# Weight slots moved 128 bytes, so that TensorE's two operands lie 64 instead of 192 bytes apart modulo 256, and the recurrence's last low part computed directly behind its gate

## The chip, the cores and the metric

The kernel runs on one core of a Trainium2 chip. The metric is the device time of one execution in microseconds (us). Before the change it is 815.14 us, the median of three runs (814.79 to 816.20 us).

## What is computed

One transformer-like block of 272 tokens (16 meta tokens and 256 others) with a model width of 1024, followed by two further layers on the 256 tokens, all in float32:

```
first_block:  a = rms_norm(h);  columns = split(a @ w_in)            # 1024 x 7680
              y_na = neighbourhood_attention(q, k, v) @ w_na_out
              y_hg = hgrn2_branch(q, z_fwd, z_bwd, i, g) @ w_hg_out  # the recurrence, both directions
              h = h + (sigmoid(gate_na)*y_na + sigmoid(gate_hg)*y_hg) @ w_o
              h = h + square(relu(rms_norm(h) @ w_up)) @ w_down
even_layer:   a, u, v, gate = split(ada(h) @ even_in);  pool mixer, spatial gating;  h += gate_res * (y @ even_out)
odd_layer:    ... = split(ada(h) @ odd_in);  gated linear attention, stick-breaking attention;  h += gate_res * (y @ odd_out)
out = rmsnorm(h)
```

The end of the recurrence branch is `o = o * rsqrt(mean(o*o)) * gain * silu(g)` per head, four heads of 128 rows. It is called the gate below. Its result is the input of `@ w_hg_out`.

## The kernel before

**Weights.** All weight matrices are cut into 259 units of 128 x 1024 numbers. SyncE's queue fetches a unit from HBM into one of six `raw` buffers. ScalarE (ACT) rounds it to TensorE's fp32r format (`wh`, the high part, line 205 of the profile, the helper `copy`), and VectorE (DVE) subtracts that from the original (`wl`, the low part, line 235, the helper `tensor_tensor`). Each activation that is multiplied is split in the same way into a high and a low part (XAh and XAl, B0h and B0l, B1h and B1l, XUh and XUl). A product is then three matmuls, Xh by wl, Xh by wh and Xl by wh, each with 128 x 128 stationary numbers and 256 moving ones per row (272 in the first stages, 258 in the stages "a" and "qk"). A full unit is 24 matmuls.

**Slots.** `wh` and `wl` have five slots (NSPLIT) of 1056 numbers, of which a unit takes 1024: it starts at the slot's number 0 or at its number 32, which is 128 bytes further. `half(j)` chooses. Unit j lies in slot j mod 5. A slot is 4224 bytes long, which is 16 times 256 and 128 more, so that neighbouring slots start 128 bytes apart modulo 256, and the choice evens that out.

**Roles.** In most stages the weights are the stationary operand and the activations move. In the stages that `streams(j)` names (the value rows v, i, vn, gv and sv) it is the other way round.

**Addresses.** From the order and the sizes of the buffers, the start addresses modulo 256 within a partition are: wh and wl 128, XAh and XAl 0, XUh, XUl, B0h, B0l, B1h and B1l 64. Most stages read XA from its number 16 on, which is at 64. So before the change a stationary weight is at 128 and the moving activation at 64: the moving operand lies 192 bytes past the stationary one modulo 256. In the `streams` stages the weights move and are at 0, the activation is stationary at 64, and the distance is again 192. Three places differ. The stage zf reads XA from its number 0 (distance 128). In the rows v the second slice of tokens starts at number 144 of XUh, which is at 128 (distance 0 - 128, or 128). In "a" and "qk" a row block of B1 or B0 is 264 numbers, 1056 bytes, long, so that the distance grows by 32 bytes with each of the eight blocks and takes all of 192, 224, 0, 32, 64, 96, 128 and 160.

**Order.** Every engine runs the same walk over the units. After each unit it takes one or two steps of a side program (attention, recurrence and others) by `next()` on a Python generator: what stands between two `yield`s is issued in one step. VectorE and ScalarE prepare the weights of a unit three and four units ahead (AHEAD, LEAD), between the steps. The order on an engine is thus fixed by the place of the `yield`s. The side program `recurrence` ends on VectorE with a loop over the four heads: the gate of head hh (`ro_gated`, line 223), the low part of the head before (`hg_low(hh - 1)`, line 235) and a `yield`; `hg_low(3)` comes behind the loop. `hg_low(hh)` waits for ScalarE's high part B0h of the same head. TensorE's stage "hg" multiplies by w_hg_out, and each of its row blocks waits for the high and the low part of one head.

Of the kernel before, what the change touches and what calls it, by code (L numbers as in the profile page):

```python
# [108 lines left out]
def bc(ap, dims):  # L109

    return bass.AP(ap.tensor, ap.offset, [list(ap.ap[0])] + [list(d) for d in dims])
# [21 lines left out]
class Counts:  # L133
# [17 lines left out]
    def up(self, name, *events):  # L151
        key = SHARE.get(name, name)
        assert self.by.setdefault(key, self.owner) == self.owner, name
        self.n[key] = self.last[name] = self.n.get(key, 0) + 1
        for ev in events:
            assert not self.known or self.value[name, ev] == self.n[key], (name, ev)
            self.value[name, ev] = self.n[key]
        return self.of(name), 1

    def at(self, name, event):  # L160
        return self.of(name), self.value[name, event] if self.known else self.value.get((name, event), 1)

    def now(self, name):
        return self.of(name), self.last[name]
# [150 lines left out]
def in_turn(*runs):  # L315

    runs = list(runs)
    while runs:
        for r in list(runs):
            try:  # L320
                next(r)
            except StopIteration:
                runs.remove(r)
                continue
            yield
# [6 lines left out]
def build(nc, ws, par, cst, msk, xt, xk, biasd, negwd, late, bsd, wtd, crd, out):  # L332
# [4 lines left out]
    with ExitStack() as ctx:  # L337
# [186 lines left out]
        def bk(*key):  # L524
            return banks[bank_of[key]] if c.known or key in bank_of else banks[0]
# [27 lines left out]
        def wide(x, g):  # L553
            return x[:, 2 * g:2 * g + 2, :]
# [16 lines left out]
        def streams(j):  # L571

            _, name, _, _, col, _ = items[mats[j]]
            return any(name == n and c0 <= col < c1 for n, c0, c1 in (
                ("w_in", 1024, 1536), ("w_in", 3072, 3584), ("even_in", 2048, 3072), ("odd_in", 1024, 2048),
                ("odd_in", 4112, 5136)))

        def half(j):
            n = j % NSPLIT
            o = 32 if n % 2 != streams(j) else 0  # L580
            return wh[:, n, o:o + 1024], wl[:, n, o:o + 1024]

        def last_unit(name, k0, c):
# [8 lines left out]
        def last_of(v, b, i):  # L592
            x = v[:, :, i:i + 1]
            return bass.AP(x.tensor, x.offset, [list(x.ap[0]), list(x.ap[1]), [0, b]])

        def halves(a, b):
            v = a.rearrange("p h (g two b) -> p (h g) two b", two=2, b=b)
            return v[:, :, 0, :], v[:, :, 1, :]
# [4 lines left out]
        def scores(b, hh):  # L603

            v = AT[:, 2 * hh:2 * hh + 2, :].rearrange("p h (a c) -> p h a c", c=128)
            return v[:, :, 1:3, :] if b == 128 else v[:, :, 0::3, :]
# [1343 lines left out]
        def vector_program(e):  # L1950
# [286 lines left out]
            def recurrence():  # L2237
                yield

                def levels(g):  # L2240
                    TF, TB = SF[g], EP[g]
                    F_, B_, KF, KB = (wide(z, g) for z in (ff, fb, kf, kb))
                    lev = -1
                    for b in LEVELS:
                        if b == 0:
                            e.tensor_tensor(Xl[g][:, :, :], KF, KB, ALU.add).then_inc(*up("xl", g))
                        elif b < 256:
                            fh, bh, tf, tb = (halves(z, b) for z in (F_, B_, TF[:, :, :], TB[:, :, :]))
                            if b == 1:
                                e.wait_ge(*at("factors", g))  # L2250
                            e.wait_ge(*at("xy", (g, b, 0)))
                            x = e.tensor_tensor(fh[1], fh[1], last_of(tf[0], b, 0), ALU.mult)
                            if b < 128:
                                x.then_inc(*up("f_new", (g, b, 0)))
                                e.wait_ge(*at("xy", (g, b, 1)))
                                e.tensor_tensor(bh[0], bh[0], last_of(tb[1], b, 0), ALU.mult).then_inc(
                                    *up("f_new", (g, b, 1)))
                                e.wait_ge(*at("k_up", (g, b)))
                                e.wait_ge(*now("f_new"))
                                for z in (tf, tb):  # L2260
                                    x = e.tensor_tensor(z[0][:, :, 0:1], z[0][:, :, 0:1], z[1][:, :, 0:1], ALU.mult)
                            x.then_inc(*up("f_up", (g, b)))
                        yield
                        if b > 64:
                            continue
                        src = bk("level", g, b)[:, :].rearrange("p (h t c) -> p h t c", h=2, t=2)
                        e.wait_ge(*at("level", (g, b)))
                        if b == 0:
                            e.wait_ge(*at("masks", 0))
                            x = e.tensor_copy(scores(b, g), src)  # L2270
                        else:
                            e.wait_ge(*now(f"at_diag"))
                            x = e.copy_predicated(scores(b, g), bc(K8[:, lev, :], [[0, 2], [0, 2], [1, 128]]), src)
                        x.then_inc(*up("at_diag", (g, b)))
                        lev += 1

                yield from in_turn(levels(0), levels(1))
                for hh in range(4):
                    e.wait_ge(*at("ro", hh))
                    e.tensor_copy(oS[hh], bk("ro", hh)[:, 0:256]).then_inc(*up("ro_copy", hh))  # L2280
                    yield
                    yield
                yield
                for hh in range(4):
                    e.wait_ge(*at("ro_normed", hh))
                    e.wait_ge(*at("silu", ("g", hh)))
                    e.scalar_tensor_tensor(oS[hh], oS[hh], hp[:, hh:hh + 1], sg[:, hh, :], ALU.mult,
                                           ALU.mult).then_inc(*up("ro_gated", hh))
                    if hh:
                        hg_low(hh - 1)  # L2290
                    yield
                hg_low(3)

            def hg_low(hh):
                low((B0h[:, 4 + hh, 0:256], B0l[:, 4 + hh, 0:256]), oS[hh], ("hg_high", hh), "hg_low", hh)

            w.side.append(recurrence())
            w.steps = 1
            rows("i", "w_in", 3072, 3584)
# [423 lines left out]
            for g in range(4):  # L2723
                b, k = g // 2, 4 * (g % 2)
                n = slice(128 * b, 128 * b + 128)
# [362 lines left out]
```

## Time and profile before

| | before |
|---|---|
| median of three runs | 815.14 us |
| the profiled execution, its own time | 816.26 us |
| its span in the profile | 814.3 us |
| TensorE busy (PE) | 800.0 us, 98% of the span |
| VectorE busy | 641.3 us, 79% |
| ScalarE busy | 501.2 us, 62% |
| GpSimd busy | 110.2 us, 14% |
| matmuls | 6996 |
| share of PE in the chain that ended last | 96% |
| granted TensorE clock, mean | 0.999 |

PE is busy in nearly every slice of the span. Since matmuls are pipelined, one lasts about 278 ns from its start to its modelled end while the next starts far earlier. The busy time therefore does not show how fast TensorE works. The distance from one start to the next does: it can be read in the timeline, or from the number of matmuls in a window.

### The profile page before, as it was taken

What the parts mean: (1) busy time and instruction counts of PE and PEld (TensorE: products, weight loads), DVE (VectorE), ACT (ScalarE), POOL (GpSimd) and SP (SyncE); (2) the same over time, 40 slices, a digit from 0 to 9 for tenths busy, and PEclk for the clock granted to TensorE, in tenths of its full rate; (3) what the DMA queues carried; (4) which work ended last, traced back from release to release, by engine and by line L of the source; (5) the groups of instructions that cost most, each with busy time, mean ns of one, the idle gap of its engine ahead of it and who ended that gap; (6) DMA issues with size and microseconds to landing.
All of it is one profiled execution on the core that took longest, in us unless ns stands there. A gap on an engine that the chain in (4) does not pass through costs nothing.

```text
span 814.3 us, 17246 instructions
## 1 busy us (share of the span) xinstructions
PE 800.0 (98%) x6996; PEld 789.3 (97%) x6996; DVE 641.3 (79%) x1032; ACT 501.2 (62%) x899; POOL 110.2 (14%) x133
## 2 busy tenths in 40 slices
PE   6999999999999999999999999999999999999996
PEld 6999999999999999999999999999999999999996
DVE  7788599977977878787998898887997568566673
ACT  6576667756567464656676844555686467566652
POOL 0022265401030000000230300001203130000001
PEclk9999999999999999999999999999999999999999
DMA  9934543566666989888777666675665446455441
GB/s 338 386 97 138 178 131 131 156 202 212 201 185 226 360 305 334 310 316 328 259 256 228 210 189 217 216 257 188 207 182 156 133 129 193 176 155 155 150 129 52
DMA packets 47021, 170.41 MB, mean 209 GB/s; under 512 B 5216, under 2 KB 5472, under 8 KB 46688
## 3 DMA queue, kind: packets, MB, share of 16 engines
q1 hardware_dynamic: 46224, 165.31, 61.5%
q10 hardware_dynamic: 720, 4.01, 1.2%
q8 instruction: 56, 0.92, 0.5%
q14 instruction: 21, 0.17, 0.1%
HBM read 168.26 MB, written 1.05 MB: 208 GB/s over the span
## 4 chain that ended last, share of the span: by engine, by line
PE 96%; DVE 1%; ACT 1%; DMA 1%; POOL 1%; issue 0%; SPq 0%; POOLq 0%; DVEq 0%; ACTq 0%
PE bank L196 95%; DMA raw<-in_ws 1%; POOL sq L235 1%; PE bank L199 0%; DVE wl L235 0%; SPq L193 0%; ACT wh L205 0%; ACT sq L202 0%; ACT B1h L202 0%; DVE gd L235 0%; DVE h L223 0%; DVE h L235 0%; POOLq L337 0%; DVEq L337 0%; DVE vt L235 0%
## 5 line engine op out<-in xcount | busy, mean ns | idle before, releaser
L235 DVE TENSOR_TENSOR wl<-raw,wh 128x1024 fp32r<-128x1024 f32 (+1 forms) x260 | 326.6, 1268 | 20.9 <-ACT wh L205 19.8
L205 ACT CAST wh<-raw 128x1024 fp32r<-128x1024 f32 (+1 forms) x260 | 269.7, 1047 | 101.4 <-PE bank L196 50.6
L196 PE MATMUL bank<-XAh,wl 128*128 128x256 f32 (+1 forms) x896 | 254.7, 284 | 0.0
L196 PE MATMUL bank<-XAl,wh 128*128 128x256 f32 (+1 forms) x896 | 249.3, 278 | 0.0
L196 PE MATMUL bank<-XAh,wh 128*128 128x256 f32 (+1 forms) x896 | 249.2, 278 | 0.0
L196 PEld LDWEIGHTS bank<-XAh,wl 128*128 128x128 f32 x896 | 168.3, 188 | 2.1 <-issue 0.7
L196 PEld LDWEIGHTS bank<-XAl,wh 128*128 128x128 f32 x896 | 168.9, 189 | 0.0
L196 PEld LDWEIGHTS bank<-XAh,wh 128*128 128x128 f32 x896 | 168.8, 188 | 0.1
L196 PE MATMUL bank<-B1h,wl 128*128 128x256 f32 (+1 forms) x464 | 129.4, 279 | 0.0
L196 PE MATMUL bank<-B1l,wh 128*128 128x256 f32 (+1 forms) x464 | 128.8, 278 | 0.0
L196 PE MATMUL bank<-B1h,wh 128*128 128x256 f32 (+1 forms) x464 | 128.8, 278 | 0.0
L235 POOL TENSOR_TENSOR sq<-sq 128x256 f32<-128x256 f32 x37 | 42.4, 1146 | 505.6 <-ACT sq L202 503.3
L196 PE MATMUL bank<-B0l,wh 128*128 128x256 f32 (+1 forms) x392 | 108.8, 278 | 0.0
L196 PE MATMUL bank<-B0h,wh 128*128 128x256 f32 (+1 forms) x392 | 108.7, 278 | 0.0
L196 PE MATMUL bank<-B0h,wl 128*128 128x256 f32 (+1 forms) x384 | 108.1, 282 | 0.0
L196 PEld LDWEIGHTS bank<-B1l,wh 128*128 128x128 f32 x464 | 87.5, 188 | 0.0
L196 PEld LDWEIGHTS bank<-B1h,wl 128*128 128x128 f32 x464 | 87.3, 188 | 0.1
L196 PEld LDWEIGHTS bank<-B1h,wh 128*128 128x128 f32 x464 | 87.3, 188 | 0.1
L196 PEld LDWEIGHTS bank<-B0h,wh 128*128 128x128 f32 x392 | 73.8, 188 | 0.1
L196 PEld LDWEIGHTS bank<-B0l,wh 128*128 128x128 f32 x392 | 73.8, 188 | 0.0
L196 PEld LDWEIGHTS bank<-B0h,wl 128*128 128x128 f32 x384 | 72.3, 188 | 0.5 <-issue 0.3
L223 DVE SCALAR_TENSOR_TENSOR raw<-raw,crow 128x1024 f32<-128x1024 f32 x48 | 58.5, 1219 | 0.0
(280 smaller groups left out, 1209.5 us busy)
## 6 DMA issues: line engine op xcount, KB each, us to landing
raw<-in_ws SPq DMA_DIRECT2D x306, 512.0 KB, 4.5
bias<-in_bias ACTq DMA_DIRECT2D x1, 1664.0 KB, 12.2
hK<-in_xk SPq DMA_DIRECT2D x4, 272.0 KB, 5.1
h<-in_xt ACTq DMA_DIRECT2D x1, 1088.0 KB, 7.4
out<-gd SPq DMA_DIRECT2D x4, 256.0 KB, 2.6
raw<-in_ws SPq DMA_DIRECT2D x2, 256.0 KB, 3.9
C<-in_cst SPq DMA_DIRECT2D x1, 512.0 KB, 8.3
crow<-in_crow ACTq DMA_DIRECT2D x1, 512.0 KB, 5.8
```

The lines of the kernel that those rows point to most:

```text
L196: return self.real.matmul(*a, **k)
L205: return self.real.copy(*a, **k)
L223: return self.real.scalar_tensor_tensor(*a, **k)
L235: return self.real.tensor_tensor(*a, **k)
```

## The change

```
 def half(j):
     n = j % NSPLIT
-    o = 32 if n % 2 != streams(j) else 0
+    o = 32 if n % 2 == streams(j) else 0
     return wh[:, n, o:o + 1024], wl[:, n, o:o + 1024]
```

Every unit now lies in the other half-place of its slot. Stationary weights are at 0 modulo 256 instead of 128, moving weights at 128 instead of 0. The distance from the stationary to the moving operand is 64 instead of 192 in both roles. In zf it becomes 0, in the second slice of the rows v also 0, and in "a" and "qk" the same eight distances come in a rotated order. No instruction is added, removed or moved by this.

```
                     if hh:
                         hg_low(hh - 1)
-                    yield
+                    if hh < 3:
+                        yield
                 hg_low(3)
```

The last `yield` of the gate's loop is gone, so `hg_low(3)` is issued in the same step as the gate of head 3 and `hg_low(2)`. On VectorE, at the end of the stage "na" and "g20", just ahead of "hg", the order of before (-) and after (+) is as follows. Xl<-Xl,hp,sg is a gate, B0l<-Xl,B0h a low part of a head, wl<-raw,wh the low part of a unit of weights, ghg<-ghg,bank the first work on a product of w_hg_out.

```order
 L235 TENSOR_TENSOR B0l<-Xl,B0h 128x256
 L223 SCALAR_TENSOR_TENSOR Xl<-Xl,hp,sg 128x256
-L235 TENSOR_TENSOR B0l<-Xl,B0h 128x256
-L235 TENSOR_TENSOR wl<-raw,wh 128x1024
-L235 TENSOR_TENSOR B0l<-Xl,B0h 128x256
-L235 TENSOR_TENSOR wl<-raw,wh 128x1024
+L235 TENSOR_TENSOR B0l<-Xl,B0h 128x256 x2
+L235 TENSOR_TENSOR wl<-raw,wh 128x1024 x2
 L223 SCALAR_TENSOR_TENSOR ghg<-ghg,bank 128x256 x2
```

The low part of head 3 has moved ahead of one low part of weights. Nothing else changes its place on any engine.

## Rows read from the trace of the kernel before

**Rows 1.** Page, parts 1 and 4: busy us; chain by engine.
```profile
PE 800.0 (98%) x6996; PEld 789.3 (97%) x6996; DVE 641.3 (79%) x1032; ACT 501.2 (62%) x899; POOL 110.2 (14%) x133
PE 96%; DVE 1%; ACT 1%; DMA 1%; POOL 1%; issue 0%; SPq 0%; POOLq 0%; DVEq 0%; ACTq 0%
```

**Rows 2.** Windows: us, busy time and (x matmuls in flight) of each engine, clock, DMA.
```profile
205.00:249.00 44.00, 44.00 (x376) 44.00 (x375) 35.58 (x58) 28.88 (x52) 8.46 (x7) 1.00 0.61 188
255.00:405.00 150.00, 150.00 (x1326) 150.00 (x1325) 122.19 (x172) 88.75 (x147) 4.02 (x3) 1.00 0.87 314
423.00:434.00 11.00, 11.00 (x94) 11.00 (x93) 10.83 (x24) 8.59 (x15) 0.00 (x0) 1.00 0.62 187
457.00:481.00 24.00, 24.00 (x206) 24.00 (x206) 23.66 (x38) 16.39 (x31) 1.80 (x2) 1.00 0.70 230
520.00:576.00 56.00, 56.00 (x497) 56.00 (x496) 46.20 (x73) 32.12 (x51) 6.12 (x5) 1.00 0.65 214
606.00:624.00 18.00, 18.00 (x161) 18.00 (x161) 16.30 (x22) 13.03 (x20) 4.93 (x5) 1.00 0.54 171
662.00:690.00 28.00, 28.00 (x249) 28.00 (x248) 22.20 (x34) 19.56 (x34) 7.15 (x8) 1.00 0.53 162
691.00:778.00 87.00, 87.00 (x720) 86.18 (x719) 55.13 (x84) 57.23 (x103) 0.00 (x0) 1.00 0.52 163
780.00:800.00 20.00, 20.00 (x179) 20.00 (x178) 11.65 (x16) 9.07 (x14) 3.21 (x3) 1.00 0.19 60
```

**Rows 3.** Timeline of PE, stage "hg" (start us, us, engine line op out<-in).
```profile
202.71 0.28 PE L196 MATMUL bank<-B0h,wl 128*128 128x256 f32 x1
...
203.27 0.28 PE L196 MATMUL bank<-B0l,wh 128*128 128x256 f32 x1
203.43 0.36 PE L196 MATMUL bank<-B0h,wl 128*128 128x256 f32 x1
203.62 0.28 PE L196 MATMUL bank<-B0h,wh 128*128 128x256 f32 x1
203.74 0.28 PE L196 MATMUL bank<-B0l,wh 128*128 128x256 f32 x1
203.86 0.28 PE L196 MATMUL bank<-B0h,wl 128*128 128x256 f32 x1
```

**Rows 4.** Timeline of DVE, the same place.
```profile
201.00 0.47 DVE L223 SCALAR_TENSOR_TENSOR Xl<-Xl,hp,sg 128x256 f32<-128x256 f32 x1
201.40 0.41 DVE L235 TENSOR_TENSOR B0l<-Xl,B0h 128x256 fp32r<-128x256 f32 x1
201.73 1.21 DVE L235 TENSOR_TENSOR wl<-raw,wh 128x1024 fp32r<-128x1024 f32 x1
202.87 0.41 DVE L235 TENSOR_TENSOR B0l<-Xl,B0h 128x256 fp32r<-128x256 f32 x1
203.20 1.21 DVE L235 TENSOR_TENSOR wl<-raw,wh 128x1024 fp32r<-128x1024 f32 x1
204.41 0.42 DVE L223 SCALAR_TENSOR_TENSOR ghg<-ghg,bank 128x256 f32<-128x256 f32 x1
```

**Rows 5.** Timeline of ACT: the high part of head 3.
```profile
201.51 0.41 ACT L205 CAST B0h<-Xl 128x256 fp32r<-128x256 f32 x1 [0.32 <-DVE Xl L223]
```

**Rows 6.** Timeline of PE, rows v: pairs of matmuls, distance 192, then 128.
```profile
34.13 0.39 PE L196 MATMUL bank<-wh,XUl 128*128 128x256 f32 x2
...
34.81 0.39 PE L196 MATMUL bank<-wh,XUl 128*128 128x256 f32 x2
35.04 0.39 PE L196 MATMUL bank<-wl,XUh 128*128 128x256 f32 x2
...
36.22 0.41 PE L196 MATMUL bank<-wh,XUl 128*128 128x256 f32 x2
```

**Rows 7.** Timeline of PE: 272 columns, distance 192 (XU), then 128 (XA in zf).
```profile
15.08 0.29 PE L196 MATMUL bank<-XUh,wh 128*128 128x272 f32 x1
...
16.56 0.29 PE L196 MATMUL bank<-XUh,wh 128*128 128x272 f32 x1
...
54.17 0.28 PE L196 MATMUL bank<-XAh,wh 128*128 128x272 f32 x1
...
55.69 0.29 PE L196 MATMUL bank<-XAh,wh 128*128 128x272 f32 x1
```

**Rows 8.** Timeline of PE where the rows vn end and the stage "ga" begins.
```profile
456.12 0.39 PE L196 MATMUL bank<-wh,XAl 128*128 128x256 f32 x2
456.35 0.28 PE L196 MATMUL bank<-XAh,wl 128*128 128x256 f32 x1
456.46 0.28 PE L196 MATMUL bank<-XAh,wh 128*128 128x256 f32 x1
456.58 0.28 PE L196 MATMUL bank<-XAl,wh 128*128 128x256 f32 x1
456.70 0.28 PE L196 MATMUL bank<-XAh,wl 128*128 128x256 f32 x1
456.82 0.28 PE L196 MATMUL bank<-XAh,wh 128*128 128x256 f32 x1
```

**Rows 9.** Page, part 5: how long the weights' preparation takes on DVE and ACT.
```profile
L235 DVE TENSOR_TENSOR wl<-raw,wh 128x1024 fp32r<-128x1024 f32 (+1 forms) x260 | 326.6, 1268 | 20.9 <-ACT wh L205 19.8
L205 ACT CAST wh<-raw 128x1024 fp32r<-128x1024 f32 (+1 forms) x260 | 269.7, 1047 | 101.4 <-PE bank L196 50.6
```

More of the change, by code:

```diff
@@ L579, in half @@
             n = j % NSPLIT
-            o = 32 if n % 2 != streams(j) else 0
+            o = 32 if n % 2 == streams(j) else 0
             return wh[:, n, o:o + 1024], wl[:, n, o:o + 1024]
```

## The prediction

> **What bounds the kernel now.** I read the page first. PE is busy for 98% of the span, and the chain that ended last is 96% PE [rows 1]. No transfer and no other engine is long on that chain, so only what changes the pace of TensorE, or makes it wait, can move the time. Busy time says nothing of the pace, so next come windows in stages with one kind of matmul. A window counts a matmul that is in flight at its edge, and one lasts 278 ns, so I take 2.4 off each count. From 255 to 405 us that leaves 1323.6 in 150 us, or 113.3 ns from start to start. The windows 520:576, 606:624, 662:690 and 780:800 give 113.2 to 113.5 [rows 2]. From 205 to 249 us it is 44 us by 373.6, or 117.8 ns, and 457:481 gives 24 by 203.6, or 117.9 [rows 2]. I call these the fast and the slow pace. The two differ by 4.5 ns, or 4%, with the same 256 columns, the same buffers, the same distance of 192 and a granted clock of 1.00 in both. The 258-column window gives 11 by 91.6, or 120.1 ns [rows 2].
>
> The timeline shows how the pace changes. In "hg" it is fast until 203.27. The next matmul starts at 203.43 and the one after it at 203.62. From there the starts are 0.12 apart [rows 3], and the window from 205 on is slow to its end. After 255 us it is fast for 150 us without a break. So a pace, once taken, is kept for long, and an interruption can change it. That is not all: at 456.46 it turns slow at the border of two stages, where no gap stands [rows 8]. The operands' addresses alone do not set it, since both paces occur at one distance.
>
> **Part one, the last low part.** Why does PE stop at 203.3? It starts the row block of head 3 there, which needs B0l of that head. VectorE ends this low part at 202.87 + 0.41 = 203.28, since 1.21 us of weights stand ahead of it (201.73) [rows 4]. The two starts from 203.27 to 203.62 take 0.35 us where two at the fast pace take 0.227, so the stop costs 0.12 us [rows 3]. In the changed order the low part comes behind the one of head 2, which ends at 201.81 [rows 4]. It waits for ScalarE's high part, which ends at 201.51 + 0.41 = 201.92 [rows 5]. It then ends near 202.4, and PE wants it at 203.3: 0.9 us to spare. The stop is gone, -0.12 us.
>
> What is queued behind the moved instruction pays. The low part of weights that began at 201.73 begins near 202.4, 0.6 us later. It is prepared three units ahead, and a unit of 24 matmuls lasts 2.7 to 2.8 us, so it has over 5 us to spare. The raw buffer that it frees is refilled 0.6 us later, with six buffers in turn. The next low part of weights (203.20) and the first ghg (204.41) come at most 0.4 us later [rows 4], since VectorE does the same work in total. The products of "hg" fill four banks and none is wanted back before "o" starts, so I cost this at nothing. Were a delay to reach PE, it would be below 0.6 us.
>
> The larger term hangs on the pace. If PE is not stopped, it should carry the fast pace through "hg", "o" and "up0", until the sum of squares at 249.3 interrupts it. From 203.6 to 249.2 are 45.6 us at 117.8 ns, or 387 matmuls. At 113.3 ns they save 387 * 4.5 ns = 1.74 us. The bounds of this term are 0 (it turns slow anyhow, as in rows 8) and -1.8.
>
> **Part two, the distance of 64.** No instruction is added. ScalarE writes and VectorE reads and writes a place 128 bytes off, for 1047 and 1268 ns a unit [rows 9]. Against a unit on PE of 2.7 us this is covered, and nothing in the trace ties those times to an address. What may change is the pace of PE. No stage runs at 64 for long, so I bound it by the nearest rows.
>
> On the side of a loss: in the rows v, matmuls at distance 192 go from 34.13 to 34.81 in 0.68 us for 6, or 113.3 ns. The next slice of tokens, at distance 128, takes from 35.04 to 36.22 for 10, or 118 ns [rows 6]. With 272 columns the distance 192 gives 1.48 / 12 = 123.3 ns and 128 gives 1.52 / 12 = 126.7 [rows 7]. So a distance can cost 3 to 5 ns. The stages "a" and "qk" go through all eight distances, 64 among them, and never reach the 114 ns that two more columns than 256 would ask for: 120.1 [rows 2]. A fast pace at full length is seen at 192 alone. If 64 never lets the fast pace come, the price is 4.5 to 6.8 ns a matmul. The fast windows of rows 2 add up to 272 us. I estimate 130 us more in stretches shared with the recurrence and both attentions, together some 3,500 matmuls: +16 to +24 us.
>
> On the side of a gain: if 64 never lets the slow pace come, the slow stretches 203.6 to 249.2 and 456.3 to 516, and an estimated half of 691:778 (720 matmuls in flight, mixed) [rows 2], are about 149 us, of which 3.8% are 5.7 us. The 1.7 us of part one are in that. The stages now at 120 ns could give up to 3 us more. So this side ends near -9 us.
>
> Between +24 and -9 I take zero, since the rows give no sign for 64. The range of whole-length windows at 192 already holds both paces, so the distance is at most one cause among several, and 64 is 192 read backwards (the stationary operand 192 past the moving one). The interruptions would then deal the paces anew, each by luck. One slow stretch of the size seen (387 matmuls, or some 500 from 456 to 516) is 1.7 to 2.3 us, so this case spreads by about 2.5 us both ways.
>
> The page "SBUF — State Buffer" of the Trainium skill says, in "Who interferes with whom", that TensorE has two independent SBUF read ports, one for the moving operand and one for the weight load. By that rule no distance could matter and only part one would be left. The step from 113.3 to 118 ns in rows 6, with nothing changed but the slice of tokens, speaks against it, though an interruption would do the same. In "TensorE: Matmul & The Clock Gate", under "Wait — 56ns, not 53.3ns?", the skill gives 2.5 ns beyond columns / 2.4 GHz, an estimate of 109.2 ns for 256 columns. The trace does not agree: 113.3 at best. By the page even the fast pace holds 4 ns of something else.
>
> **The sum.** The profiled execution took 816.26 us (span 814.3 and 2 us around it), 1.1 above the median of the runs. -0.12 for the stop, -1.74 for the pace behind it and 0 for the distance make -1.9 us: 814.4 for that execution and **813.2** against the median of 815.14.
>
> **The rivals.**
> - *64 is a bad distance.* Two reads then meet in most matmuls, and slow becomes the rule. Half of the 3,500 fast matmuls turned slow give +7.9 - 0.1 = 823 us, all of them 831, and at the pace of 120.1 it is 839. For it speak rows 6 and 7, and that 192 alone shows fast. Against it, rows 6 are one place behind an interruption. It is slower than before as soon as some 450 fast matmuls more are slow than the 387 that part one frees: one long stage.
> - *64 is a good distance.* The slow pace goes, -5.7 - 0.1 = 809.3 us, down to 806 if the stages at 120 ns gain too. For it speaks that 192 is evidently not free of the slow pace; against it, no row.
> - *Only the stop goes.* The pace turns slow at "hg" or "o" anyhow, as it does at 456.46 without a gap [rows 8], and the distance does nothing: -0.12, or 815.0 us. This is also what is left if the offset does not do what it says because the period is 128 and not 256 bytes.
>
> **How the numbers follow.** My forecast (paces dealt anew, "hg" to "up0" fast) gets 0.44, with a range of its own of 810.5 to 816. The bad distance gets 0.28, the good one 0.18, only the stop 0.10. A measurement of this kernel can tell about 0.2%, or 1.6 us, from no change, so faster means below 813.5. The forecast lies just beyond that and gives 0.28 to faster, 0.11 to the same and 0.05 to slower. With the good distance faster is 0.46. With only the stop the same is 0.21. With the bad distance slower is 0.33. The range is 806.5 to 831. It leaves out the half of the bad case at which the pace falls below 117.8 (about 0.1) and little at the lower end.
>
> **What would show it.** Step one is right if the DVE timeline shows B0l of head 3 ending near 202.4 and PE has no gap at 203.3. Step two is right if a window from 205 to 249 us holds about 390 matmuls instead of 376. The distance is neutral if the window of 150 us in "up" and "down" still holds about 1326, and the slow stretches elsewhere are as long as before, though in other places. It is a bad distance if that window falls to 1275 (slow) or 1250 (120 ns), and a good one if 457:481 rises from 206 to 214. The prediction is wrong if the stretch between 250 and 400 us changes its pace, since then the distance and not the interruptions decides.

## The result, and the profile after

The changed kernel takes 830.89 us, the median of four runs (830.67 to 831.31), against 815.11 us for the kernel before on the same chip. The ratio on record is 1.0176, with a 95% interval from 1.0135 to 1.0217 (the two medians by themselves give 1.0194). The forecast of 813.2 us was wrong. What came is the rival "64 is a bad distance" at the price it had with all fast matmuls turned slow, 831 us, which was the upper end of the range.

The profiled execution took 831.03 us with a span of 829.0 us, 14.7 us more than the span before. Of the page, first the busy times of part 1, then the chain of part 4, then the two lines on the weights' preparation:

```profile
PE 815.2 (98%) x6996; PEld 804.6 (97%) x6996; DVE 641.9 (77%) x1032; ACT 499.3 (60%) x899; POOL 110.3 (13%) x133
PE 98%; DMA 0%; POOL 0%; DVE 0%; ACT 0%; issue 0%; SPq 0%; DVEq 0%; ACTq 0%; POOLq 0%
L235 DVE TENSOR_TENSOR wl<-raw,wh 128x1024 fp32r<-128x1024 f32 (+1 forms) x260 | 326.7, 1268 | 22.8 <-ACT wh L205 21.7
L205 ACT CAST wh<-raw 128x1024 fp32r<-128x1024 f32 (+1 forms) x260 | 268.4, 1042 | 106.4 <-PE bank L196 58.7
```

Against [rows 1] PE has the same 6996 matmuls and is busy for 15.2 us longer. The other engines do the same work in the same time. The preparation of the weights takes 1268 and 1042 ns a unit, as in [rows 9]. So no longer wait shows there, and TensorE itself is slower. The windows, with the columns of [rows 2], say where:

```profile
205.00:249.00 44.00, 44.00 (x376) 44.00 (x375) 36.35 (x60) 27.98 (x48) 8.49 (x7) 1.00 0.62 193
255.00:405.00 150.00, 150.00 (x1276) 150.00 (x1275) 115.63 (x165) 84.98 (x146) 0.17 (x1) 1.00 0.86 310
457.00:481.00 24.00, 24.00 (x209) 24.00 (x208) 21.18 (x33) 18.50 (x34) 5.80 (x7) 1.00 0.66 210
520.00:576.00 56.00, 56.00 (x476) 55.95 (x476) 44.77 (x76) 29.53 (x46) 1.57 (x1) 1.00 0.64 212
662.00:690.00 28.00, 28.00 (x233) 27.79 (x233) 18.93 (x28) 17.63 (x29) 7.97 (x9) 1.00 0.50 146
780.00:800.00 20.00, 20.00 (x168) 19.89 (x167) 16.50 (x28) 11.02 (x16) 0.00 (x0) 1.00 0.52 158
```

The 150 us of "up" and "down" hold 1276 matmuls where [rows 2] have 1326. With 2.4 taken off, that is 150 / 1273.6 = 117.8 ns from start to start, the slow pace, at a granted clock of 1.00 as before. The windows 520:576, 662:690 and 780:800 fall from 497, 249 and 179 to 476, 233 and 168. That is more than the pace alone, since each stage now begins 8 to 14 us later and part of such a window lies in the stage ahead of it. By the start stamps the stages themselves run at 117.8 ns, without a break from 525 to 587 and from 792 to 817 us. Those that were slow before stay as they were: 205:249 holds 376 again, and 457:481 goes from 206 to 209, since it is fast up to 464.4 us.

From the start stamps of the whole trace, by the mean of three neighbours: of some 5,600 matmuls by weights with 256 columns, about 4,000 ran at 113 to 115 ns before and 1,300 at 117 to 119. After the change it is about 620 and 4,700. The mean of the 5,500 steps that hold no stop (below 150 ns) goes from 114.59 to 117.29 ns, and 2.70 ns * 5,500 = 14.9 us, which is the whole difference of the spans. Matmuls with 258 columns (120.3 and 120.2 ns) and with 272 (125.7 and 126.0) have no part in it.

The end of the recurrence on DVE and the high part on ACT, with the columns of [rows 4] and [rows 5], then PE at the same place:

```profile
202.79 0.47 DVE L223 SCALAR_TENSOR_TENSOR Xl<-Xl,hp,sg 128x256 f32<-128x256 f32 x1
203.19 0.97 DVE L235 TENSOR_TENSOR B0l<-Xl,B0h 128x256 fp32r<-128x256 f32 x2
204.07 1.22 DVE L235 TENSOR_TENSOR wl<-raw,wh 128x1024 fp32r<-128x1024 f32 x1
```

```profile
203.29 0.41 ACT L205 CAST B0h<-Xl 128x256 fp32r<-128x256 f32 x1 [0.33 <-DVE Xl L223]
```

```profile
203.55 0.28 PE L196 MATMUL bank<-B0h,wh 128*128 128x256 f32 x1
203.66 0.28 PE L196 MATMUL bank<-B0l,wh 128*128 128x256 f32 x1
203.78 0.28 PE L196 MATMUL bank<-B0h,wl 128*128 128x256 f32 x1
...
204.49 0.28 PE L196 MATMUL bank<-B0h,wl 128*128 128x256 f32 x1
```

The last two low parts now stand in one row of DVE, x2, and end at 204.16, 0.46 us behind the high part. PE goes on in steps of 0.12 us with no stop like the one in [rows 3]. It has nothing to lose there, since it was slow already.

### The profile page after: what moved, and what is told of

Its sections match the earlier page's. It is cut to its first block, busy times and chain, and to the rows that moved or that the text cites. A ratio compares the mean times of both kernels' runs of the same rounds, so it can differ in the third digit from the quotient of the medians.

```text
span 829.0 us, 17246 instructions
## 1 busy us (share of the span) xinstructions
PE 815.2 (98%) x6996; PEld 804.6 (97%) x6996; DVE 641.9 (77%) x1032; ACT 499.3 (60%) x899; POOL 110.3 (13%) x133
## 4 chain that ended last, share of the span: by engine, by line
PE 98%; DMA 0%; POOL 0%; DVE 0%; ACT 0%; issue 0%; SPq 0%; DVEq 0%; ACTq 0%; POOLq 0%
PE bank L196 97%; DMA raw<-in_ws 0%; PE bank L199 0%; POOL sq L235 0%; DVE gd L235 0%; ACT B1h L202 0%; SPq L193 0%; DVEq L337 0%; ACT sq L202 0%; DVE wl L235 0%; ACT wh L205 0%; DVE h L235 0%; DVE h L223 0%; ACT rsB L202 0%; ACT lnb L202 0%
## 5 line engine op out<-in xcount | busy, mean ns | idle before, releaser
L235 DVE TENSOR_TENSOR wl<-raw,wh 128x1024 fp32r<-128x1024 f32 (+1 forms) x260 | 326.7, 1268 | 22.8 <-ACT wh L205 21.7
L205 ACT CAST wh<-raw 128x1024 fp32r<-128x1024 f32 (+1 forms) x260 | 268.4, 1042 | 106.4 <-PE bank L196 58.7
```

The costliest lines, as they stand in the source:

```text
L205: return self.real.copy(*a, **k)
L235: return self.real.tensor_tensor(*a, **k)
```

## The experiments

Ratios are those on record, against runs of the kernel before on the same chip. They are not the quotients of the two medians, and differ from them by up to 0.4%. A pace is the mean time from one matmul's start to the next.

**The two parts apart.** *low_only* undoes the flip of the slots and keeps the low part behind its gate:

```
-            o = 32 if n % 2 == streams(j) else 0
+            o = 32 if n % 2 != streams(j) else 0
```

> Only the last low part of the recurrence is moved behind its gate; the distance stays at 192. Theory A (the distance of 64 makes the slow pace of 117.8 ns the rule, the low part only removes a stop): the stop of 0.12 us at 203.3 goes, and the fast pace of 113.3 ns is carried on to 249 us, 813.2 us, about 1.9 below before; a window from 205 to 249 us holds about 390 matmuls. Rival B (the pace turns slow at this place anyhow): about 815.0 us, 376 matmuls. Rival C (the changed order of VectorE is what made the changed kernel slower): 825 us or more.

It took 814.62 us (814.28 to 815.31, 11 runs) against 814.87, ratio 0.999 (0.9972 to 1.0008). Its DVE, its PE and two windows:

```profile
201.33 0.47 DVE L223 SCALAR_TENSOR_TENSOR Xl<-Xl,hp,sg 128x256 f32<-128x256 f32 x1
201.72 0.98 DVE L235 TENSOR_TENSOR B0l<-Xl,B0h 128x256 fp32r<-128x256 f32 x2
202.62 2.35 DVE L235 TENSOR_TENSOR wl<-raw,wh 128x1024 fp32r<-128x1024 f32 x2
```

```profile
203.28 0.28 PE L196 MATMUL bank<-B0l,wh 128*128 128x256 f32 x1
203.39 0.28 PE L196 MATMUL bank<-B0h,wl 128*128 128x256 f32 x1
203.50 0.28 PE L196 MATMUL bank<-B0h,wh 128*128 128x256 f32 x1
```

```profile
205.00:249.00 44.00, 44.00 (x389) 43.95 (x388) 37.06 (x61) 29.99 (x54) 8.48 (x7) 1.00 0.60 199
255.00:405.00 150.00, 150.00 (x1326) 150.00 (x1325) 122.01 (x175) 87.11 (x144) 4.68 (x3) 1.00 0.87 314
```

In the trace this is the first part as predicted: the low part is done by 202.7, the stop is gone and the fast pace goes on through "hg", 389 matmuls where 376 were. The profiled span is 812.8 against 814.3 us, -1.5 us. The time is not as predicted. The medians differ by 0.25 us, within their interval, where 1.9 us were expected. The next pair of kernels shows why.

*dist64_only* is the complement. It keeps the flip and puts the last `yield` back.

> Only the slots are moved, so that the distance is 64; the low part stays in its old place. Theory A (the distance makes the loss): 830 to 832 us, window 255 to 405 us with about 1276 matmuls. Rival C (the loss needs the moved low part): about 815 us.

It took 830.95 us (ratio 1.0197, 1.0181 to 1.0212), with 1276 matmuls from 255 to 405 us, as expected. The flip alone does all the damage.

**Place or distance.** The flip also moves the weights. *acts_moved_64* leaves them at 128 and moves the activations by 128 bytes, which gives a distance of 64. *both_moved_192* has both the flip and the shift, and so a distance of 192 with the weights at 0. Both kernels keep the last `yield` where it was before the change. The shift:

```
         wl = sbt(ctx, "wl", [128, NSPLIT, 1056], F32R)
+        sbt(ctx, "shift", [128, 32])
         XAh = sbt(ctx, "XAh", [128, 8, 320], F32R)
```

> The weights stay where they are before the change (stationary at 128 modulo 256), but all buffers behind them, the activations among them, lie 128 bytes further, so that the distance from the stationary to the moving operand is 64. Theory A (the distance counts): as slow as the changed kernel, 829 to 833 us. Rival D (the absolute place of the weights at 0 instead of 128 counts, for instance for the engines that write them): 815 us.

> Weights at their new place (stationary at 0 modulo 256) and all buffers behind them 128 bytes further too, so that the distance is again 192. Theory A (the distance counts): 812 to 818 us, with the fast pace of 113.3 ns in most of the window 255 to 405 us. Rival D (the absolute place counts): 829 to 833 us.

They took 830.84 us (1.0194, 1.018 to 1.0208) and 814.83 us (1.0001, 0.9975 to 1.0027), with 1276 and 1326 matmuls in the long window. Between these four pairs of places, 128 bytes apart, the distance decides and the place does not.

*both_moved_192* also answers the question that *low_only* left. It has the old order on DVE, and so the stop of PE at head 3, here at 203.94 us. Yet the stretch behind the stop is fast:

```profile
203.81 0.28 PE L196 MATMUL bank<-B0l,wh 128*128 128x256 f32 x1
203.94 0.36 PE L196 MATMUL bank<-B0h,wl 128*128 128x256 f32 x1
204.13 0.28 PE L196 MATMUL bank<-B0h,wh 128*128 128x256 f32 x1
205.00:249.00 44.00, 44.00 (x388) 43.95 (x388) 36.78 (x61) 29.64 (x53) 8.47 (x7) 1.00 0.63 196
```

The last line is the window with the columns of [rows 2]: 388 matmuls, as many as *low_only* has without the stop. So the stop does not by itself make this stretch slow. The profiled execution of the kernel before, 816.26 us, was slow there. *both_moved_192* was fast there at 815.12, and most executions of the kernel before lie near 814.9. That they were fast in this stretch too is inferred, since none of them was profiled. It would explain why taking the stop away leaves the median as it is.

**Which stages.** *stationary_64* has `o = 32 if n % 2 == 0 else 0`, which gives 64 to the stages with stationary weights alone. *moving_64* has `n % 2 == 1`, which gives it to the rows alone.

> Only the stages in which the weights are stationary get the distance 64 (the slots start at their number 32 in slots 0, 2 and 4 for every unit); the rows stages keep 192. Theory A1 (the loss is all in the stages with stationary weights, since the rows vn and gv ran at 113.3 ns at 64 in the changed kernel's trace): 830 to 832 us. Rival (each stage loses by its share of the matmuls, the rows stages hold about an eighth): 828 to 829 us.

> Only the rows stages, in which the weights move, get the distance 64; all others keep 192. Theory A1: 814 to 816 us, no change. Rival (share of the matmuls): about 817 us.

*stationary_64* took 831.64 us (1.02, 1.0183 to 1.0217), so the stages with stationary weights hold the loss. *moving_64* took 814.68 us (0.9998, 0.9964 to 1.0033). Its profiled execution took 821.86 us, and shows something else:

```profile
255.00:405.00 150.00, 150.00 (x1276) 150.00 (x1275) 117.25 (x164) 84.49 (x141) 1.37 (x1) 1.00 0.85 307
```

"up" and "down" lie at 192 in this kernel, and here they ran at 117.8 ns from 249.7 to 416.3 us, 1,414 matmuls with 256 columns, behind the sum of squares at 249.2. 1,414 * 4.5 ns = 6.4 us, most of the 7.2 us to its median. So 192 does not secure the fast pace. The kernel before has such executions too. Its runs lie at some 814 to 817 or at 822 to 824, and in one set of runs 13 of 22 were in the upper group. No execution of it in the upper group was profiled, so that its cause is the same is inferred from *moving_64*.

Other slow stretches do not change from kernel to kernel. By the stamps the 214 matmuls from about 456 to 481 us are slow in the kernel before, *low_only*, *both_moved_192* and *place32_192* alike, and so are 44 matmuls near 492 and 68 near 508. In *moving_64* the rows "vn" ahead of the first of them lie at 64, and there it is fast (463 to 487 us). That is one execution, and it suggests that what stood before has a part in the choice.

**Other distances in the kernel.** *dist0*, *dist128* and *dist32* use the shift with 16, 16 (with the flip) and 24 numbers.

> The slots as before, and all buffers behind the weights 64 bytes further, so that both operands start at the same place modulo 256 (distance 0). Theory A (a place of its own for each distance; 192 is the good one): between 819 and 840 us, since the second slice of the rows v and zf ran at 118 and 126.7 ns at 128. Rival E (only odd and even multiples of 64 differ, or the period is 128): 0 behaves as 128 does, and 64 as 192, which the changed kernel has already spoken against. Rival F (any distance but 64 is as good as 192): about 815 us.

> The slots of the changed kernel and all buffers behind the weights 64 bytes further: distance 128. If the pace that TensorE has alone at a distance carries over to the kernel (118.67 ns at 128 against 120.00 at 0, where the kernel took 844.0 us, with some 5,000 matmuls at that pace), it takes 844.0 - 5,000 * 1.33 ns = 837 us. If the kernel's other engines matter as well, it is off this by more than 2 us.

> The slots as before the change and all buffers behind the weights 96 bytes further: distance 32. By the pace alone (116.69 ns) 844.0 - 5,000 * 3.31 ns = 827 us, faster than the changed kernel at 64 (117.78) and slower than before. If other engines matter as well, it is off this by more than 2 us.

| distance | us | ratio (interval) | matmuls in 255:405 | pace, ns |
|---|---|---|---|---|
| 192 | 814.8 | 1 | 1326 | 113.3 |
| 64 | 830.9 | 1.0176 (1.0135 to 1.0221) | 1276 | 117.8 |
| 32 | 830.85 | 1.0158 (1.0037 to 1.028) | 1289 | 116.6 |
| 128 | 840.59 | 1.0277 (1.0154 to 1.0401) | 1265 | 118.8 |
| 0 | 843.96 | 1.0351 (1.0335 to 1.0366) | 1252 | 120.0 |

All lose. *dist32* and *dist128* came 3.9 and 3.6 us above what was expected of them from lone paces. The order of 0, 128 and 32 was right, the sizes were not, and 32 was not faster than 64 as expected: it is so in the long window (1289 against 1276), but the whole kernel takes the same.

**TensorE alone.** *pace_alone* runs the same matmuls with no other engine at work and zeros as the output. A section has one distance, and an interruption stands ahead of each.

```
off = (XO + d // 4) % 64          # d: the section's distance in bytes
for k in range(4):
    for b in range(2):
        s = slice(256 * k + 128 * b, 256 * k + 128 * b + 128)
        m = slice(off + 320 * k, off + 320 * k + 256)
        for st, mv in ((wl, Xh), (wh, Xh), (wh, Xl)):
            e.matmul(ps[:, 256 * b:256 * b + 256], st[:, s], mv[:, m], ...)
```

> TensorE alone, computing nothing of the reference (the output is filled with zeros): units of 24 matmuls of 256 columns as in the kernel, at the distances 192, 64, 0, 128, 224, 96, 32 and 160, 192 matmuls each behind an interruption by two plain float32 matmuls, all of it twice, then the rows pattern (two halves for each stationary block) at the same distances. Theory A2 (TensorE's own two reads of SBUF meet, no other engine is needed): 113.3 ns or less at 192, 117.8 ns at 64, and some distances near 120. Rival G (the reads of VectorE and ScalarE are what it meets): the same pace at all eight distances, 109 to 113 ns.

Windows inside the sections for 192, 64, 0, 32, and 192 a second time:

```profile
15.50:34.50 19.00, 19.00 (x170) 19.00 (x169) 0.00 (x0) 0.00 (x0) 0.00 (x0) 1.00 0.00 1
38.00:57.00 19.00, 19.00 (x163) 19.00 (x163) 0.00 (x0) 0.00 (x0) 0.00 (x0) 1.00 0.00 1
61.50:80.50 19.00, 19.00 (x160) 19.00 (x160) 0.00 (x0) 0.00 (x0) 0.00 (x0) 1.00 0.00 1
156.50:175.50 19.00, 19.00 (x165) 19.00 (x165) 0.00 (x0) 0.00 (x0) 0.00 (x0) 1.00 0.01 2
203.50:222.50 19.00, 19.00 (x163) 19.00 (x163) 0.00 (x0) 0.00 (x0) 0.00 (x0) 1.00 0.01 2
```

With DVE, ACT and POOL at 0.00 the paces are the kernel's own: 113.4, 118.3, 120.6, 116.9 ns by these counts (113.3, 117.8, 120.0 and 116.7 by the stamps). The last window is 192 again, now slow. So the pace is a matter of TensorE and its two operands. Accesses by other engines are not needed for it, and one distance can have two paces.

*pace_scan* went through all distances in steps of 16 bytes, each behind four interruptions, and then gave 192 and 64 another 24 interruptions each. *pace_choice* put units at other distances ahead of the section.

> TensorE alone again, computing nothing of the reference (the output is zeros). First every distance from 0 to 240 in steps of 16 bytes, each behind four interruptions of different length, 72 matmuls each; then 192 and 64 in turn behind 24 interruptions of different length (a plain float32 matmul of 256 columns and one of 16 to 246). Theory A3 (192 has two paces and the interruption picks one; 64 has only the slow one): at 192 between 5 and 20 of the 24 are at 113.3 ns and the others at 117.8, at 64 none or nearly none is at 113.3; each other distance has one pace of its own, between 116 and 120.2 ns. Rival H (64 has both paces too, and the kernel only happened to pick the slow one at its few interruptions): about as many of the 24 at 113.3 for 64 as for 192.

> TensorE alone, computing nothing of the reference (the output is zeros): the distances 64, 192 and 112, each behind one unit at the distance 48, 192, 64 or 112 and an interruption of six lengths, 48 matmuls each; then rows of 258 and 272 columns at six distances. Theory A5 (64 has both paces, but the fast one is taken only behind some distances before the interruption, such as 48, and never behind 192 or 64): at 64 fast in 3 or more of 6 behind 48, in none behind 192 and 64; at 192 fast in most of all; at 112 fast in all 24. Rival J (the distance before does not matter, only the interruption's length): the same answer behind all four for each length. For 258 columns about 120 ns at every distance, since the kernel's stages a and qk kept 120.1 to 120.3 ns at all; for 272 columns 123.3 ns at 192 and 126.7 at 128.

By the start stamps, with the stationary operand at 128: only 64, 112 and 192 reached 113.3 ns. In the scan 64 and 192 had it in three of four sections and 117.8 in one, and 112 in four of four. In the 24 further sections 192 had it in 18 and 64 in none. In *pace_choice* it was 5 of 24 for 64, 6 of 24 for 192 and 24 of 24 for 112. All other distances gave 116.6 to 120.1, and 16, 80 and 128 had two paces of their own. So 64 does have a fast pace. Theory A3 gave it none and fell with the first scan. Rival H fell with the 24 sections, in which 192 was fast 18 times and 64 never. A5 and J fell in *pace_choice*: behind 48, 192, 64 and 112 the distance 64 was fast 2, 0, 2 and 1 times of six, and 192 1, 2, 2 and 1 times. Which pace is taken follows no rule that I found.

The end of *pace_choice* missed as well. Rows of 258 columns did not run at about 120 ns at every distance: it was 118.7 at 64 and 112, 119.9 at 32, 120.0 at 0, 120.9 at 192 and 122.2 at 128. With 272 columns it was 123.3 at 192, 126.7 at 64, 112 and 128, 125.3 at 0 and 125.7 at 32. So the best distance is another one for each width.

**Distance 112 in the kernel.** It looked like a cure. *dist112* sets it by other slots, in all stages with stationary weights:

```
+            o = 1024 * n + 4                       # weights at 144 modulo 256
+            return wh[:, o:o + 1024], wl[:, o:o + 1024]
```

> The distance 112 in all stages with stationary weights (slots of 1024 numbers that start 16 bytes past 128 modulo 256, buffers behind the weights moved to fit), with the last low part behind its gate; the rows stages then lie at 144. Alone, TensorE ran at 113.3 ns at 112 behind all four interruptions and at 118.65 at 144. Theory A4 (112 has only the fast pace, in the kernel too): the 900 or so slow matmuls of stages with stationary weights in the kernel with the low part alone gain 4.5 ns each, -4 us; the 770 matmuls of the rows stages that were fast lose 5.3 ns each, +4 us: 813 to 816 us, the windows 457 to 516 us fast instead of slow. Rival I (112 only happened to be fast behind those four interruptions): slow stretches at 112 as at 192, 818 us or more.

It took 842.46 us (ratio 1.03, 1.0245 to 1.0355), with

```profile
255.00:405.00 150.00, 150.00 (x1252) 150.00 (x1252) 113.91 (x159) 83.08 (x141) 0.00 (x0) 1.00 0.84 300
```

120.0 ns, as at distance 0. The theory that 112 is fast in the kernel too (A4) fell. The lone runs had the stationary operand at 128, this kernel at 144. *pace_place* therefore moves both operands on together:

```
-            def unit(n, d, cols=256):
-                off = (XO + d // 4) % 64
+            def unit(n, d, at=0):
+                w0 = at // 4                     # the stationary operand starts at 128 + at
+                off = (XO + (d + at) // 4) % 64
```

> TensorE alone, zeros as output; sections of two units of 24 matmuls with 256 columns, each behind a unit at distance 64 and an interruption (widths 256, 200, 144, 88). First at distance 112, then at 192; within each both operands are moved on together by 0, 16, 32, 64, 112, 128, 144, 192 and 240 bytes, so that the stationary one starts at 128, 144, 160, 192, 240, 0, 16, 64 and 112 modulo 256. Measured: mean time from start to start. Theory A6 (the place itself counts, beside the distance): 112 gives 113.3 ns in four of four at 128, the place of the earlier lone runs, and a slower pace, 118 to 120, at 144, the place of the kernel with 112 that took 842 us; 192 is alike at 0 and 128 (the two places of the kernels with 192 that took 814.8), with 113.3 in some of four and 117.8 in others. Theory B6 (only the distance counts): 112 gives 113.3 in all 36 sections, and the kernel with 112 was slow from something that the lone runs lack (other engines' accesses, stages at 144, gaps).

The pace from the 13th matmul of each section on, in ns:

| stationary operand at (modulo 256) | distance 112 | distance 192 |
|---|---|---|
| 0, 64, 128, 192 | 113.3 in 16 of 16 | 113.3 in 8 of 16, else 117.8 |
| 160 | 113.3 in 4 of 4 | 113.3 in 4 of 4 |
| 16, 112, 144, 240 | 120.0 in 15 of 16, 118.3 in one | 113.3 in 16 of 16 |

The 7th and the 43rd matmul of a section at distance 112, with the stationary operand at 128 and then at 144:

```profile
17.22 0.28 PE L68 MATMUL bank<-Xh,wl 128*128 128x256 f32 x1
...
21.33 0.28 PE L68 MATMUL bank<-Xh,wl 128*128 128x256 f32 x1
...
62.70 0.28 PE L68 MATMUL bank<-Xh,wl 128*128 128x256 f32 x1
...
67.01 0.28 PE L68 MATMUL bank<-Xh,wl 128*128 128x256 f32 x1
```

4.11 and 4.31 us for 36 steps, or 114.2 and 119.7 ns, the first steps of a section included, in which neither pace is steady yet. Theory A6 held. The place counts after all, modulo 32: at places that are 16 past a multiple of 32, distance 112 loses its fast pace, and distance 192 its slow one. The steps of 128 bytes in the first experiments could not show this. (All places are worked out from the order and sizes of the buffers, with the first taken to start at 128. No trace shows an address.)

**The place in the kernel.** *place16_192* has distance 192 and moves weights and activations on by 16 bytes (views that start four numbers further, in buffers laid together so that they fit), weights at 144 and activations at 80. *place32_192* moves everything by 32 bytes. *place16_64* is *place16_192* with the flip. All three have the low part behind its gate.

```
-        wl = sbt(ctx, "wl", [128, NSPLIT, 1056], F32R)
-        XAh = sbt(ctx, "XAh", [128, 8, 320], F32R)
+        wlx = sbt(ctx, "wlx", [128, 5280 + 2560], F32R)
+        wl = wlx[:, 4:5284].rearrange("p (s n) -> p s n", n=1056)
+        XAh = wlx[:, 5280:7840].rearrange("p (k n) -> p k n", n=320)[:, :, 4:320]
...                                             # XAl, XU, B0 and B1 likewise
```

> Distance 192 as before, with the low part behind its gate, and weights and activations both moved on by 16 bytes: stationary weights at 144 modulo 256, moving activations at 80. TensorE alone ran at distance 192 with the stationary operand at 16 modulo 32 at 113.3 ns in 16 of 16 sections, and at 0 modulo 32 in 12 of 20. Theory A7 (the place of the lone runs carries over): the slow pace goes. The kernel with only the low part moved took 814.6 us and holds some 860 slow matmuls by the estimate from the kernel before; 860 * 4.5 ns = 3.9 us, so 810.7 us (809 to 812), no execution near 822, windows 457:481 at 214 and 255:405 at 1326. Theory B7 (in the kernel the place does not count): 814.7 us, with some executions near 822. Theory C7 (the place counts otherwise than in the lone runs, as a new distance did): slower, 820 to 843.

> Distance 192, low part behind its gate, every buffer moved on by 32 bytes: stationary weights at 160 modulo 256, moving activations at 96. TensorE alone was at 113.3 ns there in 4 of 4 sections, against 1 of 4 at 128. Theory A7: the slow pace goes, 810.7 us (809 to 812). Theory B7: 814.7 us, with some executions near 822. Theory D7 (only an odd multiple of 16 bytes cures it, and 4 of 4 was luck): as B7.

> The changed kernel (distance 64, low part behind its gate) with weights and activations both moved on by 16 bytes: stationary weights at 16, moving activations at 80. The lone runs did not try 64 at such a place. Theory A8 (the distance of 64 itself is slow): 831 us, 255:405 with 1276. Theory B8 (whether the slow pace comes is a matter of the place, and 16 modulo 32 frees 64 of it as it freed 192): 811 us, 255:405 with 1326. The loss of the change would then be one of distance and place together.

*place16_192* took 811.55 us (811.16 to 812.22, 11 runs). *place32_192* took 814.71 us (814.39 to 815.46, 12 runs), and *place16_64* 828.20 us (827.33 to 828.89, 4 runs). The kernel before took 822.39 in the median of the same set, with 13 of its 22 runs above 821, so the ratios on record mix its two times: 0.9901 (0.9869 to 0.9933), 0.9941 (0.9911 to 0.9971) and 1.0111 (1.0057 to 1.0165). Against the median of its nine other runs, 815.09, the medians give 0.9957, 0.9995 and 1.0161. For *place16_192* that is theory A7. For *place32_192* it is B7 or D7 in time, though no run of it was near 822. Two windows of *place16_192*, with the same two of *place32_192* below:

```profile
457.00:481.00 24.00, 24.00 (x214) 24.00 (x213) 23.55 (x40) 14.40 (x26) 1.69 (x2) 1.00 0.71 222
606.00:624.00 18.00, 18.00 (x174) 17.81 (x174) 13.79 (x18) 12.93 (x20) 6.25 (x6) 1.00 0.59 186
```

```profile
457.00:481.00 24.00, 24.00 (x207) 24.00 (x206) 23.55 (x40) 14.52 (x26) 1.69 (x2) 1.00 0.73 222
606.00:624.00 18.00, 18.00 (x170) 17.87 (x170) 14.99 (x19) 12.58 (x20) 6.25 (x6) 1.00 0.57 172
```

At the place 16 bytes on, 457:481 holds the 214 that the prediction named as the sign of a good distance. By the stamps the slow matmuls (three-neighbour mean of 117.4 to 118.2) number some 125 in *place16_192*, against some 800 in *low_only*: 675 * 4.5 ns = 3.0 us, and the medians differ by 3.1. To *place32_192*, in the same set of runs, it is 3.2. How it comes about shows behind an interruption in *place16_192* (wlx is the buffer that now holds wl and XAh):

```profile
497.83 0.50 PE L196 MATMUL bank<-wT,vn 128*128 128x128 f32 x3
498.08 0.36 PE L196 MATMUL bank<-wlx 128*128 128x256 f32 x1
498.28 0.28 PE L196 MATMUL bank<-wlx,wh 128*128 128x256 f32 x1
...
498.99 0.28 PE L196 MATMUL bank<-wlx,wh 128*128 128x256 f32 x1
499.11 0.28 PE L196 MATMUL bank<-XAl,wh 128*128 128x256 f32 x1
499.22 0.28 PE L196 MATMUL bank<-wlx 128*128 128x256 f32 x1
...
500.24 0.28 PE L196 MATMUL bank<-wlx 128*128 128x256 f32 x1
```

From 498.28 to 498.99 six steps take 0.71 us, 118 ns each. From 499.11 to 500.24 ten take 1.13, 113 ns. At this place the slow pace comes too, and lapses after six or seven matmuls. In the 16 lone sections at such places the fast one was there after 2 to 9 steps. At a multiple of 32 distance 192 was fast by the sixth step in 12 of 20 lone sections, and slow to the end in the other 8. *place32_192*, at such a place, still has 800 slow matmuls, so the 4 of 4 at 160 in the table were luck or do not carry over. At distance 64 the 16 bytes did not help "up" and "down" (1270 matmuls in 255:405), and the whole kernel gained only 2.7 us. The loss of the change is thus one of the distance 64, at both places.

## Why the prediction was wrong

**What bounds the kernel** stood: TensorE's pace and nothing else. The two paces, 4.5 ns apart, come back in the kernels and in the lone runs at distance 192. The slow stretch that begins at 456.46 without a stop [rows 8] is slow in *low_only* too. In *place16_192* the slow pace begins at the same border and lapses there after five or six matmuls (454.35 to 454.94 us).

**Part one, the last low part,** was right in its order of events and wrong in its size. *low_only* has the low part done by 202.7 (forecast 202.4), no stop, and 389 matmuls in 205:249 (forecast about 390). What was queued behind the moved instruction delayed nobody. But the median fell by 0.25 us (interval of the ratio 0.9972 to 1.0008), where the sum has -1.86. The step that failed is "If PE is not stopped, it should carry the fast pace through", with -1.74 us. *both_moved_192* is stopped there and goes on fast, with 388 matmuls in 205:249. The forecast had read the price of the stop from one execution, 1.1 us above the median, and then took it off the median.

**Part two failed** too, and far more heavily, at the step "Between +24 and -9 I take zero, since the rows give no sign for 64". The term measured +16.1 us (*dist64_only* against 814.87). Two arguments led there. One was that 64 is 192 read backwards, so that both should behave alike. The lone runs show what is true of it: both have the same two paces, 113.3 and 117.8. How often each is taken differs in *pace_scan* (192 fast 18 times of 24, 64 never) and not in *pace_choice* (6 and 5 times of 24). In the kernels with stationary weights at 64, at a multiple of 32, "up" and "down" were slow in all four profiles, as was every other long stretch with stationary weights. Why the kernel takes the slow pace of 64 so regularly is open. The other argument was that interruptions deal the paces by luck. They do not deal evenly, since the slow stretches near 456, 492 and 508 us come back in four kernels. And what is dealt is held for long: one slow choice at 249 us costs some 6.4 us, as the execution of *moving_64* shows. The spread of 2.5 us that I gave to my own case was taken from stretches of 387 to 500 matmuls, and left out that of 1,324.

**The signs for the bad distance.** That a second slice of tokens at 128 went at 118 ns [rows 6], and that 192 alone was ever seen fast at full length, were listed and given a chance of 0.28. The second deserved more: in the lone scan 13 of 16 distances are slow always, so an unknown one is likelier to be slow than to be as good as the best. The reading of "a" and "qk" was no sign either way. Alone, 258 columns ran at 120.9 ns at 192 itself, and at 118.7 at 64, so the 120.1 of these stages [rows 2] says little of 256 columns at any distance. The mechanism that the rival named, two reads that meet, is not shown by any run. The runs show that the pace depends on both addresses.

**The price of the rival** was sound: "all of them 831" used 3,500 matmuls * 4.5 ns = 16 us. The count by stamps gives about 3,400 turned slow.

**The rule of two ports.** The lone runs give 113.3, 117.8 and 120.0 ns by the distance of two operands, with every other engine idle. The page "SBUF — State Buffer" of the Trainium skill ("Who interferes with whom") calls the two read ports of TensorE, for the moving operand and for the weight load, independent. The prediction took from this that the distance could not matter, and the measurement does not agree with that. Whether the ports or something behind them makes the difference, no run shows.

## What to carry to other kernels

Where TensorE bounds a kernel with long runs of fp32r matmuls, measure the time from start to start and treat the operands' start addresses as a tuning parameter: here they were worth up to 3.5% one way and 0.4% the other, with no instruction changed. Test the distance modulo 256, the place modulo 32 and the width together, in the kernel itself: distance 112 was fast alone at one place, and 27 us slower than before in the kernel at another. Where single executions differ, price an effect against the execution that is near the median, or profile more than one. Cost an address that no stage uses by what the tried ones mostly show, not by the best one.

## What the hardware showed

- The pace of the same fp32r matmul with 256 columns lies between 113.3 and 120.0 ns, depending on where its two operands start (*pace_scan*, with values such as 116.7, 117.8, 118.4 and 118.7 between), at a granted clock of 1.00.
- At distance 192 there are two paces, 113.3 and 117.8 ns, and either was kept for some 1,400 matmuls, until the stage ended (the kernel before and *moving_64*). With operands 16 bytes past a multiple of 32 the slow one ends by itself within ten matmuls (*pace_place*, *place16_192*).
- A kernel can thus have two times without any change: some 814 to 817 and 822 to 824 us for the kernel before. *place16_192* had no second time in 11 runs, *place32_192* none in 12, though it holds some 800 slow matmuls, and *low_only*, at the old place, none in 11. What the three share is the low part behind its gate. With the stationary weights at distance 192 and the old order, the second time came in 25 of 95 runs (the kernel before, *both_moved_192*, *moving_64*). Whether the order keeps it away is not tested, since no kernel at the new place had the old order.
- Open is what in TensorE or its memory makes the pace depend on both addresses, and why an interruption at 192 or 64 leads to the one pace or the other. No kernel was tried with distance 112 and weights at a multiple of 32.
